# In the first attention, VectorE takes the low part of a step's transposed rows ahead of the maximum that belongs to two steps on

## The chip, the cores and the metric

The program runs on one core of one Trainium2 chip. A core has a matrix engine (PE, TensorE), a vector engine (DVE, VectorE), a scalar engine (ACT, ScalarE), GpSimd (POOL) and a queue engine (SP). Each works through its own list of instructions in order, and they wait for one another by semaphores. The metric is the device time of one execution in microseconds (us), median over runs; less is faster.

## The reference, cut to what matters

Two blocks follow one another on 512 tokens of width 1024, the first with 256 context tokens beside them. The change touches only the first attention of the first block, which has 8 heads, keys of 96 columns (64 computed for each head, 32 shared and rotated) and values of 64:

```python
def attention(q, k, v):
    ...
        s = jnp.einsum('bqhgd,bkhd->bhgqk', qi, k).astype(jnp.float32) * scale
        p = jax.nn.softmax(s, axis=-1).astype(v.dtype)
        return jnp.einsum('bhgqk,bkhd->bqhgd', p, v)

def mla_pool_mixer(hc, hl, w_in, g_q, w_uq, g_kv, w_uk, w_uv, w_pool, s_pool, w_out, cos, sin, need_ctx):
    ...
    al = attention(ql, jnp.concatenate([kc, kl], axis=1), jnp.concatenate([vc, vl], axis=1))
    ...
        ac = attention(qc, kc, vc)
```

The 512 main tokens attend to all 768 keys, the 256 context tokens to the 256 context keys. Everything is computed in 32-bit precision.

## The kernel before, in words

**Products in two parts.** Each 32-bit operand of a matmul is held as a high part, which ACT writes (`copy`, line 1317), and a low part, which DVE writes as the value less its high part (`low`, line 1866). `three` (lines 620 to 622) then makes three matmuls. Weight tiles (`RAW`) are split in the same way: ACT writes `WH`, DVE writes `WL` (`split`, line 1859). There are two slots for weight tiles, and PE waits until both parts of a tile are there (`tile_ready`).

**Steps.** The first attention has 8 heads (numbered 0 to 7 here) of 5 steps (0 to 4), 40 in all, counted by `w`. Step 0 of a head has the two query blocks of the context side by side (2 x 256 columns); steps 1 to 4 have 128 queries by 768 keys each. A step goes through these hands:

- `scores(w)` on PE, issued two steps ahead (in step w-2),
- `maximum(w)` on DVE (line 2120), also issued two steps ahead,
- `exps(w)` on ACT (line 1466), two steps ahead as well: it waits for the maximum,
- `prob(w)` on DVE, one step ahead: reciprocal of the sum (line 2126) and scaling (line 2129),
- `transposes(w)` on PE (line 841), then `pt_high_of(w)` on ACT and `pt_low(w)` on DVE, which copy the transposed rows out as high and low part (`PTA`),
- `values(x)` on PE with the finished rows, and `out_taken(x)` on ACT, which copies its result out (`OA_C`, `OA_M`).

**What else stands in the steps.** While one head runs, the next head's operands are made: in step 0 `context_products`, in step 1 the queries and their rotation (`query_rope` on DVE, four long instructions, lines 2073 to 2078), in step 2 the keys (`key_high`, `key_low`) and the halves of the rotated queries (`query_high` on ACT, behind `exps`; `query_low` on DVE), in steps 3 and 4 of odd heads the values. In steps 3 and 4 of even heads ACT and DVE split the two weight tiles of the next pair of heads; on both engines the split is the last thing of its step. In the odd head's step 0, `context_products` on PE waits for both tiles.

Beside that run pieces of the modulation (steps 2 and 4 of heads 0 to 6, steps 1 to 4 of head 7): PE makes `mod_rows` (line 634), DVE copies the sums out (`mod_take`, line 1871, tile `MROW`), PE turns them (`mod_turn`, line 642) and DVE adds them (`mod_add`, line 1876). On PE `mod_rows` stands ahead of the step's transposes and waits for an `out_taken`, since they share a PSUM bank; `mod_turn` stands behind the transposes, and the next step's `scores` stand behind it. The order on every engine is written out by hand.

ACT's order in a step is: `out_taken` (steps 1, 2 and 4), the copies for the next head, `pt_high_of(w)`, `exps(w + 2)`, then `query_high` (step 2) or the tile split (steps 3 and 4 of even heads).

Of the kernel before, what the change touches and what calls it, by code (L numbers as in the profile page):

```python
# [98 lines left out]
def build(nc, a, out):  # L99
# [118 lines left out]
    with ctx:  # L218
# [179 lines left out]
        MLA_UNITS = MLA_HEADS * MLA_STEPS  # L398
# [11 lines left out]
        def mla_row(w):  # L410
            return psf[:, 1024 * (w % 2) + TC:1024 * (w % 2) + 1024]
# [4 lines left out]
        def mla_pt(w, pt):  # L416

            n, x = w % MLA_STEPS, mla_x(w)
            flat = psf[:, 4 * 512:4 * 512 + (4 if n == 0 else 6) * P]
            if n == 0:  # L420
                return (pt[:, x % 2, 0:2, :].rearrange("p b (q n) -> p q b n", q=2), flat.rearrange("p (q b n) -> p q b n", q=2, b=2))
            q = (n - 1) % 2
            return pt[:, x % 2, :, q * P:(q + 1) * P], flat.rearrange("p (b n) -> p b n", b=6)
# [7 lines left out]
        def mla_widths(w):  # L431
            return (TC, TC) if w % MLA_STEPS == 0 else (TA,)
# [3 lines left out]
        def mla_mod_sums(bank):  # L436
            return PS[:, bank, 2 * P:4 * P]

        def mla_mod_col(bank):
            return PS[:, bank, 0:4]  # L440
# [1414 lines left out]
        def _(dve):  # L1855
            def split(s):

                dve.wait_ge(tile_hi, s.times(1, 1))
                dve.tensor_tensor(WL[:, s.mod(2), :], RAW[:, s.mod(2), :], f32(WH[:, s.mod(2), :]), ALU.subtract  # L1859
                                  ).then_inc(tile_split[s.mod(2)], 1)  # L1860
# [4 lines left out]
            def low(dst, src, high):  # L1865
                return dve.tensor_tensor(dst, src, f32(high), ALU.subtract)  # L1866

            def mod_take(j, sums=MOD_SUMS):

                dve.wait_ge(mod_done, j.times(2, 2))  # L1870
                dve.tensor_copy(MROW[:, :], sums).then_inc(mod_row, 1)

            def mod_add(j, col=MOD_COL):

                dve.wait_ge(mod_turned, j.times(1, 1))
                dve.tensor_tensor(MOD[:, j.ds(2, 2), :], col.rearrange("p (a v) -> p a v", a=2),
                                  COLS[:, j.ds(2, 2, COL["b_mod"])].unsqueeze(2).to_broadcast([P, 2, 2]), ALU.add).then_inc(mod_read, 1)
# [213 lines left out]
            def context_low(j):  # L2091
                dve.wait_ge(mla_ctx_hi, j + 1)
                low(QA[1][rows96, j % 2, 0:TC], PS[rows96, ctx_bank(j), 0:TC], QA[0][rows96, j % 2, 0:TC])
                low(KA[1][rows64, j % 2, 0:TC], PS[rows64, ctx_bank(j), TC:2 * TC], KA[0][rows64, j % 2, 0:TC]).then_inc(mla_ctx_read, 1)

            def key_low(j):
                dve.wait_ge(mla_k_hi, j + 1)
                low(KA[1][rows64, j % 2, TC:TA], PS[rows64, key_bank(j), :], KA[0][rows64, j % 2, TC:TA]).then_inc(mla_k_read, 1)

            def query_rope(j):  # L2100
                dve.wait_ge(mla_q_read, j + 1)
                if j:
                    dve.wait_ge(mla_q_ready, j)
                rope(At(1 + j), rows96, QRAW_A[rows96, :], RT[0][rows96], rope_done)

            def query_low(j):
                dve.wait_ge(mla_q_hi, j + 1)
                low(QA[1][rows96, j % 2, TC:TA], RT[0][rows96], QA[0][rows96, j % 2, TC:TA]).then_inc(mla_q_ready, 1)

            def value_low(pair, half):  # L2110
                dve.wait_ge(mla_v_hi, 2 * pair + half + 1)
                hi, lo = [x[:, 3 * half:3 * half + 3, :].rearrange("p b n -> p (b n)") for x in VA[pair % 2]]
                low(lo, value_bank(pair, half), hi).then_inc(mla_v_read, 1)

            def maximum(w):

                dve.wait_ge(score_done, w + 1)
                n = len(mla_widths(w))
                src = mla_row(w)[:, 0:sum(mla_widths(w))].rearrange("p (n k) -> p n k", n=n)
                dve.tensor_reduce(STAT[:, w % 2, 0:n], src, AX.X, ALU.max, negate=True).then_inc(row_max, 1)  # L2120

            def prob(w):

                dve.wait_ge(row_exp, w + 1)
                st, n, at = STAT[:, w % 2, :], len(mla_widths(w)), 0
                dve.reciprocal(st[:, 4:4 + n], st[:, 2:2 + n]).then_inc(row_recip, 1)
                dve.wait_ge(row_recip, w + 1)
                for m, width in enumerate(mla_widths(w)):
                    ins = dve.tensor_scalar(PROB[:, w % 2, at:at + width], PROB[:, w % 2, at:at + width], st[:, 4 + m:5 + m], None, ALU.mult)
                    at += width  # L2130
                ins.then_inc(row_prob, 1)

            def pt_low(w):
                dve.wait_ge(pt_hi, w + 1)
                hi, flat = mla_pt(w, PTA[0])
                lo, _ = mla_pt(w, PTA[1])
                low(lo, flat, hi).then_inc(pt_ready, 1)

            def out_low(i):
                dve.wait_ge(mla_out_hi, i + 1)  # L2140
                low(GC[1][:, i, :], OA_C[:, i, :], GC[0][:, i, :])
                low(GM[1][:, i, :], OA_M[:, i, :], GM[0][:, i, :]).then_inc(mla_out_ready, 1)
# [11 lines left out]
            for w in range(MLA_UNITS):  # L2154
                j, n = w // MLA_STEPS, w % MLA_STEPS
                more = j + 1 < MLA_HEADS
                if w + 1 < MLA_UNITS:
                    prob(w + 1)
                if w + 2 < MLA_UNITS:
                    maximum(w + 2)  # L2160
                if more:
                    if n == 0:
                        context_low(j + 1)
                    elif n == 2:
                        key_low(j + 1)
                    elif n >= 3 and j % 2:
                        value_low((j + 1) // 2, n - 3)
                if w in MLA_PAIR:
                    pair, bank = MLA_PAIR[w]
                    mod_take(At(pair), mla_mod_sums(bank))  # L2170
                pt_low(w)
                if w in MLA_PAIR:
                    mod_add(At(pair), mla_mod_col(bank))
                if more:
                    if n == 1:
                        query_rope(j + 1)
                    elif n == 2:
                        query_low(j + 1)
                    elif n >= 3 and j % 2 == 0:
                        split(At(TILES["mla"] + j + n - 1))  # L2180
                elif n < 3:
                    out_low(n)
# [634 lines left out]
```

## Time and profile before

| | us |
|---|---|
| median of 3 runs | 3115.05 |
| the three runs | 3099.72, 3115.77, 3115.05 |
| the profiled execution | 3100.32 |
| its span | 3098.6 |
| PE busy in the span | 2781.3 (90%) |
| DVE busy | 1625.6 (52%) |
| ACT busy | 1052.9 (34%) |
| steps of the first attention, from about 205 to 431 | 226 |

The profile is of one execution. A timeline row gives the start, the duration, the engine, the line, the operation and its tiles; in square brackets stands how long the engine sat idle before it and what ended that. Rows that follow at once on an engine overlap by a few hundredths, since a record runs from start to finish of a pipelined instruction. The whole first attention is 7% of the span; the rest of the program isn't touched.

### The profile page before, as it was taken

How to read it: one execution, taken by the hardware profiler on the slowest of the kernel's cores; microseconds unless marked ns; L12 is line 12 of the kernel's file. 1: busy time of each engine (PE TensorE's matmuls, PEld its weight loads, DVE VectorE, ACT ScalarE, POOL GpSimd, SP SyncE). 2: the span in 40 equal slices, each digit the busy share in tenths (PEclk: the TensorE clock that was granted, in tenths of full speed). 3: DMA queues.
4: the chain of work that ended last, by engine and by line, in shares of the span. 5: the costliest groups of instructions: out<-in, count | busy, mean ns of one | idle time of the engine just before them, and what ended most of it. 6: DMA issues, size and time to landing. Idle time of an engine off the chain costs nothing. (4 is left out here: it accounts for less than half of the span.)

```text
span 3098.6 us, 38172 instructions
## 1 busy us (share of the span) xinstructions
PE 2781.3 (90%) x14558; PEld 2236.1 (72%) x14558; DVE 1625.6 (52%) x2409; ACT 1052.9 (34%) x1620; POOL 82.0 (3%) x108
## 2 busy tenths in 40 slices
PE   5968987999999977887899997989997999999997
PEld 3857776888888866776677775777774777777775
DVE  5576645333333347675544445255555565555566
ACT  2144433222222223453333333333333333333343
POOL 0000110000000000000000000000000000000000
PEclk8989998999999998999899998989998999999999
DMA  5212231222222211001122222212221222222221
GB/s 202 68 55 83 82 116 54 96 96 88 95 95 88 95 62 41 29 21 55 61 89 88 88 88 102 90 63 78 81 81 56 82 84 84 84 77 84 84 77 41
DMA packets 67206, 246.41 MB, mean 80 GB/s; under 512 B 7505, under 2 KB 7889, under 8 KB 66385
## 3 DMA queue, kind: packets, MB, share of 16 engines
q1 hardware_dynamic: 51280, 185.10, 18.1%
q0 software_dynamic: 14768, 55.51, 5.4%
q10 hardware_dynamic: 1040, 4.12, 0.4%
q8 instruction: 89, 1.46, 0.2%
q14 instruction: 29, 0.23, 0.0%
HBM read 242.45 MB, written 2.24 MB: 79 GB/s over the span
## 5 line engine op out<-in xcount | busy, mean ns | idle before, releaser
L1859 DVE TENSOR_TENSOR WL<-RAW,WH 128x1024 fp32r<-128x1024 f32 x331 | 405.2, 1225 | 696.4 <-ACT WH L1317 693.9
L620 PE MATMUL PS<-HM,WH 128*128 128x512 f32 x1752 | 707.7, 404 | 32.4 <-DVE HM L1866 10.9
L621 PE MATMUL PS<-HM,WH 128*128 128x512 f32 x1752 | 700.3, 400 | 0.0
L622 PE MATMUL PS<-HM,WL 128*128 128x512 f32 x1752 | 698.6, 399 | 0.0
L1317 ACT ACTIVATE WH<-RAW 128x1024 fp32r<-128x1024 f32 x331 | 349.5, 1057 | 776.1 <-PE PS L622 765.9
L620 PEld LDWEIGHTS PS<-HM,WH 128*128 128x128 f32 x1752 | 333.4, 190 | 111.0 <-issue 32.3
L622 PEld LDWEIGHTS PS<-HM,WL 128*128 128x128 f32 x1752 | 333.4, 190 | 80.1
L621 PEld LDWEIGHTS PS<-HM,WH 128*128 128x128 f32 x1752 | 333.6, 190 | 55.1
L620 PE MATMUL PS<-GM,WH 128*128 128x512 f32 x468 | 192.0, 410 | 27.2 <-DVE GM L1866 15.5
L621 PE MATMUL PS<-GM,WH 128*128 128x512 f32 x468 | 191.4, 409 | 0.0
L622 PE MATMUL PS<-GM,WL 128*128 128x512 f32 x468 | 190.7, 407 | 0.0
L620 PE MATMUL PS<-HC,WH 128*128 128x256 f32 x448 | 132.6, 296 | 36.6 <-DVE HM L1918 28.9
L620 PEld LDWEIGHTS PS<-HC,WH 128*128 128x128 f32 x448 | 85.6, 191 | 73.5 <-issue 40.0
L622 PE MATMUL PS<-HC,WL 128*128 128x256 f32 x448 | 129.8, 290 | 0.0
L621 PE MATMUL PS<-HC,WH 128*128 128x256 f32 x448 | 127.9, 286 | 0.0
L620 PEld LDWEIGHTS PS<-GM,WH 128*128 128x128 f32 x468 | 92.0, 197 | 42.8 <-DVE GM L1866 18.2
L2193 DVE SCALAR_TENSOR_TENSOR X_M<-PS,MOD,X_M 128x512 f32<-128x512 f32 x112 | 83.5, 746 | 68.5 <-PE PS L622 68.5
L622 PEld LDWEIGHTS PS<-GM,WL 128*128 128x128 f32 x468 | 91.5, 196 | 22.1
L2193 DVE SCALAR_TENSOR_TENSOR X_C<-PS,MOD,X_C 128x256 f32<-128x256 f32 x56 | 27.1, 483 | 149.8 <-PE PS L622 149.8
L1866 DVE TENSOR_TENSOR PTA<-PS,PTA 128x768 fp32r<-128x768 f32 (+1 forms) x72 | 66.4, 923 | 71.7 <-ACT PTA L1317 71.6
L1773 ACT ACTIVATE PROB<-PROB,STAT 128x768 f32<-128x768 f32 x64 | 59.5, 931 | 128.7 <-DVE STAT L2553 128.7
L1317 ACT ACTIVATE PTA<-PS 128x768 fp32r<-128x768 f32 (+1 forms) x72 | 56.6, 787 | 125.9 <-PE PS L1040 80.4
(357 smaller groups left out, 4787.7 us busy)
## 6 DMA issues: line engine op xcount, KB each, us to landing
RAW<-in_tiles SPq DMA_DIRECT2D x333, 512.0 KB, 3.3
MRAW<-in_mods POOLq DMA_DIRECT2D x80, 512.0 KB, 4.6
TB<-bias_rows POOLq DMA_DIRECT2D x16, 576.0 KB, 6.3
FIRST<-in_mods SPq DMA_DIRECT2D x8, 1024.0 KB, 23.8
X_M<-in_x ACTq DMA_DIRECT2D x1, 2048.0 KB, 17.0
VN_GB<-in_gm_rows POOLq DMA_DIRECT2D x2, 1024.0 KB, 5.9
out_x<-X_M SPq DMA_DIRECT2D x8, 256.0 KB, 2.0
X_C<-in_ctx ACTq DMA_DIRECT2D x1, 1024.0 KB, 19.8
```

Of the source, the lines that this page charges most:

```text
L620: pe.matmul(out_, wh, xh, start=first, stop=False, skip_group_check=True)
L621: pe.matmul(out_, wh, xl, start=False, stop=False, skip_group_check=True)
L622: return pe.matmul(out_, wl, xh, start=False, stop=last, skip_group_check=True)
L1317: return act.activation(out_, in_, ACT.Copy, scale=scale)
L1773: act.activation(rows, rows, ACT.Exp, bias=STAT[:, h, 0:1], accum_out=STAT[:, h, 2:3]).then_inc(dil_exp, 1)
L1859: dve.tensor_tensor(WL[:, s.mod(2), :], RAW[:, s.mod(2), :], f32(WH[:, s.mod(2), :]), ALU.subtract).then_inc(tile_split[s.mod(2)], 1)
L1866: return dve.tensor_tensor(dst, src, f32(high), ALU.subtract)
L2193: return dve.scalar_tensor_tensor(out=xx, in0=src, scalar=MOD[:, col.ds(), v:v + 1].rearrange("p a v -> p (a v)"), in1=xx, op0=ALU.mult, o ...
```

## The change

`maximum(w + 2)` moves from behind `prob(w + 1)` to behind `pt_low(w)`. No instruction is added or removed, and only DVE's order changes.

```diff
@@ the loop over the steps, on VectorE @@
                 if w + 1 < MLA_UNITS:
                     prob(w + 1)
-                if w + 2 < MLA_UNITS:
-                    maximum(w + 2)
                 if more:
                     if n == 0:
                         context_low(j + 1)
...
                     mod_take(At(pair), mla_mod_sums(bank))
                 pt_low(w)
+                if w + 2 < MLA_UNITS:
+                    maximum(w + 2)
                 if w in MLA_PAIR:
                     mod_add(At(pair), mla_mod_col(bank))
```

VectorE's list in the first head, from `mod_take` of step 2 to the end of step 3. Line 2120 is the maximum, 1871 `mod_take`, 1866 with `PTA` is `pt_low`, 1866 with `QA` is `query_low`, 2126 and 2129 are `prob`, 1859 is the low part of a weight tile. Before:

```order
L1871 COPY MROW<-PS 128x256
L1866 TENSOR_TENSOR PTA_109<-PS,PTA_108 128x6x128
L1876 TENSOR_TENSOR MOD<-PS,COLS 128x4
L1866 TENSOR_TENSOR QA_107<-RT_113,QA_106 96x512
L2126 RECIPROCAL STAT<-STAT 128x1
L2129 TENSOR_SCALAR PROB<-PROB,STAT 128x768
L2120 TENSOR_REDUCE STAT<-PS 128x2
L1866 TENSOR_TENSOR PTA_109<-PS,PTA_108 128x6x128
L1859 TENSOR_TENSOR WL<-RAW,WH 128x1024
```

The same stretch after:

```order
L1871 COPY MROW<-PS 128x256
L1866 TENSOR_TENSOR PTA_109<-PS,PTA_108 128x6x128
L2120 TENSOR_REDUCE STAT<-PS 128x1
L1876 TENSOR_TENSOR MOD<-PS,COLS 128x4
L1866 TENSOR_TENSOR QA_107<-RT_113,QA_106 96x512
L2126 RECIPROCAL STAT<-STAT 128x1
L2129 TENSOR_SCALAR PROB<-PROB,STAT 128x768
L1866 TENSOR_TENSOR PTA_109<-PS,PTA_108 128x6x128
L2120 TENSOR_REDUCE STAT<-PS 128x2
L1859 TENSOR_TENSOR WL<-RAW,WH 128x1024
```

The maximum of step 4 (`128x1`) now stands between step 2's `pt_low` and `query_low`, and that of the next head's step 0 (`128x2`) between step 3's `pt_low` and the weight tile. Step 4 of the same head on VectorE, up to the reciprocal of the step that follows. Before:

```order
L2120 TENSOR_REDUCE STAT<-PS 128x1
L1871 COPY MROW<-PS 128x256
L1866 TENSOR_TENSOR PTA_109<-PS,PTA_108 128x6x128
L1876 TENSOR_TENSOR MOD<-PS,COLS 128x4
L1859 TENSOR_TENSOR WL<-RAW,WH 128x1024
```

After:

```order
L1871 COPY MROW<-PS 128x256
L1866 TENSOR_TENSOR PTA_109<-PS,PTA_108 128x6x128
L2120 TENSOR_REDUCE STAT<-PS 128x1
L1876 TENSOR_TENSOR MOD<-PS,COLS 128x4
L1859 TENSOR_TENSOR WL<-RAW,WH 128x1024
```

The maximum went from ahead of `mod_take` to between `pt_low` and the weight tile.

## Rows read from the trace of the kernel before

**Rows 1.** The head of the page.
```profile
span 3098.6 us, 38172 instructions
```
**Rows 2.** Waits of PE from 205 to 431: us in total, times, longest.
```profile
PE PS L642 <- DVE MROW L1871: 21.2, 12, 2.4
PE PS L620 <- issue: 4.5, 3, 1.6
```
**Rows 3.** Timeline of DVE in head 4, steps 1 and 2.
```profile
325.27 0.96 DVE L1866 TENSOR_TENSOR PTA<-PS,PTA 128x768 fp32r<-128x768 f32 x1 [2.68 <-ACT PTA L1317]
...
329.73 0.94 DVE L2120 TENSOR_REDUCE STAT<-PS 128x1 f32<-128x768 f32 x1
...
331.19 0.40 DVE L1871 COPY MROW<-PS 128x256 f32<-128x256 f32 x1
```
**Rows 4.** Timeline of PE in head 4, steps 2 to 4, and after.
```profile
331.64 0.61 PE L642 MATMUL PS<-CONST,MROW 128*128 128x2 f32 x4 [2.36 <-DVE MROW L1871]
...
338.43 1.04 PE L634 MATMUL PS<-MRAW,CVEC 128*2 128x256 f32 x16
...
344.38 0.33 PE L620 MATMUL PS<-CQ,WH 128*96 128x256 f32 x1 [1.59 <-issue]
```
**Rows 5.** Timeline of ACT in head 4, steps 2 to 4.
```profile
330.70 0.90 ACT L1466 ACTIVATE PROB<-PS,STAT 128x768 f32<-128x768 f32 x1 [0.51 <-DVE STAT L2120]
...
331.59 0.62 ACT L1317 ACTIVATE QA<-RT 96x512 fp32r<-96x512 f32 x1
...
335.82 0.47 ACT L1466 ACTIVATE PROB<-PS,STAT 128x256 f32<-128x256 f32 x1
...
336.71 1.06 ACT L1317 ACTIVATE WH<-RAW 128x1024 fp32r<-128x1024 f32 x1
337.66 0.37 ACT L1317 ACTIVATE OA_M<-PS 64x256 f32<-64x256 f32 x1
340.38 0.81 ACT L1317 ACTIVATE PTA<-PS 128x768 fp32r<-128x768 f32 x1 [2.35 <-PE PS L841]
341.09 0.89 ACT L1466 ACTIVATE PROB<-PS,STAT 128x768 f32<-128x768 f32 x1
...
341.96 1.05 ACT L1317 ACTIVATE WH<-RAW 128x1024 fp32r<-128x1024 f32 x1
```
**Rows 6.** Timeline of DVE in head 4, steps 2 to 4.
```profile
332.45 0.67 DVE L1866 TENSOR_TENSOR QA<-RT,QA 96x512 fp32r<-96x512 f32 x1
...
333.23 0.62 DVE L2129 TENSOR_SCALAR PROB<-PROB,STAT 128x768 f32<-128x768 f32 x1
333.77 0.69 DVE L2120 TENSOR_REDUCE STAT<-PS 128x2 f32<-128x512 f32 x1
335.95 0.96 DVE L1866 TENSOR_TENSOR PTA<-PS,PTA 128x768 fp32r<-128x768 f32 x1 [1.49 <-ACT PTA L1317]
...
343.05 1.23 DVE L1859 TENSOR_TENSOR WL<-RAW,WH 128x1024 fp32r<-128x1024 f32 x1 [0.80 <-ACT WH L1317]
```
**Rows 7.** Timeline of head 0: `mod_take` of step 2, and PE's next context products.
```profile
216.78 0.41 DVE L1871 COPY MROW<-PS 128x256 f32<-128x256 f32 x1
...
228.41 0.33 PE L620 MATMUL PS<-CQ,WH 128*96 128x256 f32 x1 [1.32 <-issue]
```
**Rows 8.** Timeline of DVE in head 3, step 4.
```profile
313.46 0.56 DVE L1866 TENSOR_TENSOR VA<-PS,VA 128x384 fp32r<-128x384 f32 x1 [1.52 <-ACT VA L1317]
313.94 0.42 DVE L1871 COPY MROW<-PS 128x256 f32<-128x256 f32 x1
```
**Rows 9.** Stretches: length; busy PE, PEld, DVE, ACT, POOL; PEclk; DMA share; GB/s.
```profile
327.50:331.60 4.10, 1.78 (x22) 0.88 (x22) 4.02 (x8) 2.30 (x5) 1.44 (x2) 1.00 0.35 107
332.10:335.50 3.40, 3.40 (x18) 3.40 (x18) 2.33 (x6) 0.50 (x2) 0.00 (x0) 0.51 0.33 129
```
**Rows 10.** Timeline of PE in head 7, steps 2 and 3.
```profile
410.67 1.89 PE L634 MATMUL PS<-MRAW,CVEC 128*2 128x256 f32 x16 [0.15 <-ACT OA_C L1317]
...
416.19 0.61 PE L634 MATMUL PS<-MRAW,CVEC 128*2 128x256 f32 x8 [1.75 <-DMA MRAW<-in_mods]
```

## The prediction

> **What bounds the kernel now.** The profiled execution took 3100.3 us, its span is 3098.6 [rows 1]. I read the waits of PE over the first attention first, because PE is the busiest engine and because what follows the attention starts when PE is through with it. Its largest wait there is for `MROW`, the sums that `mod_take` on DVE copies out: 21.2 us in 12 waits [rows 2]. The second is called "issue", 4.5 us in three waits of up to 1.6. In the timeline such a wait stands ahead of the context products that follow an even head [rows 4] (at 344.38), and it ends 0.10 after DVE's low part of the second weight tile (343.05 + 1.23 = 344.28) [rows 6]. It is a wait for that tile. So in even heads two things of DVE hold PE: `mod_take` and the tile.
>
> **What the change seems to offer, and why it isn't there.** Before, a maximum (0.86 us in a queue, 0.94 less the overlap with its neighbour) stands ahead of `mod_take`, and PE waits 2.36 us for `mod_take` in step 2 of a head [rows 3, 4]. Taking the maximum out should give 0.86 in each of seven heads. But follow DVE back from that `mod_take`. It worked without a gap from the low part of step 1, which itself began after 2.68 us of idleness, when ACT's high part was done (at 325.27) [rows 3]. Between this anchor and `mod_take` stand the rotation, `prob`, one maximum (at 329.73) and the low part of the keys. After the change the maximum of step 2 is gone from there, but that of step 1, which used to lie in the 2.68 us of idleness, now comes right behind the low part of step 1. One maximum leaves and one enters: `mod_take` of step 2 stays where it is. Gain 0, in all seven heads with this pattern.
>
> **What it costs: `exps` comes behind two more instructions.** Before, ACT took `exps(w+2)` directly behind its high part, since the maximum was long there (the high part at 340.38 ends at 341.19, `exps` starts at 341.09) [rows 5]. Now DVE first takes the low part (0.88) and then the maximum (0.87), and everything behind `exps` in ACT's list comes later: `query_high` in step 2, the tile in steps 3 and 4, `out_taken` of the next step. The low parts on DVE wait for the first two, and `mod_rows` on PE waits for the last. I follow this from the end of `mod_take` in step 2 of head 4 (331.59) to PE's context products:
>
> - low part of step 2, 0.88, and maximum, 0.86 [rows 3, 6]: 1.74
> - `exps` and `query_high` on ACT, from 330.70 to 332.21 in [rows 5], and 0.03 to begin: 1.54
> - `query_low` on DVE [rows 6]: 0.70; `prob`, from the end of the former at 333.12 to 333.85: 0.73
> - low part of step 3, 0.88, and the two-part maximum, 0.69 less 0.08 [rows 6]: 1.49. The low part would start at 336.3; the high part that it needs was there at 335.95 in this trace [rows 6], so DVE's queue is what counts.
> - `exps`, tile and `out_taken` on ACT, from 335.82 to 338.03 [rows 5]: 2.24. This is the place that I consider the heart of it: `mod_rows` of step 4 on PE waits for this `out_taken`.
> - `mod_rows`, transposes, high part: from 338.43 [rows 4] to 341.19 [rows 5], and 0.05: 2.81
> - low part of step 4, 0.99, and maximum, 0.87: 1.86
> - `exps` and tile on ACT, from 341.09 to 343.01 [rows 5]: 1.95
> - low part of the tile, 1.27, and 0.10 to PE: 1.37
>
> The sum is 16.43 us. Before, the same stretch took 344.38 - 331.59 = 12.79 in head 4, and in head 0 228.41 - 217.19 = 11.22 [rows 7]. Head 0 is quicker because PE's clock was not at half there, as it was in head 4 from 332.1 to 335.5 [rows 9]; the new chain runs mostly through ACT and DVE, so I take it as the same 16.43 for both. Cost: 5.2 in head 0, 3.6 in head 4, and 3.6 in head 2, which shows the same tile wait. Together 12.5. Within it PE's `mod_turn` of step 4 comes some 1.2 later than before; that is part of the sum, not beside it.
>
> **Odd heads** have no tile in steps 3 and 4. DVE waits there for the values from PE and ACT, 1.52 us before 313.46, and `mod_take` follows that [rows 8]. The moved maximum and the later `exps` (about 1.9 us) fit ahead of it: 0, at most 0.5 in each of three heads.
>
> **Head 6 and head 7.** After head 6 no context products follow, so PE doesn't wait for a tile but, in head 7, for `out_taken` behind ever later `exps`. At least one low part and one maximum go on the path: 1.8. At most, `mod_rows` of step 2 moves by 5.4 (from 410.67 [rows 10], by the same adding up: 3.6 from the tile of head 6, the rest from low part and maximum in steps 0 and 1). It now waits for ACT's copy by only 0.15. Behind it PE waits 1.75 for a transfer of modulation weights that is issued when `mod_rows` frees the buffer, so that moves too, and is not a cover. Since the slow clock there (1.89 for rows that take 1.04 elsewhere) may fall away, I take 4.5.
>
> **The clock.** In head 4 PE was busy 1.78 of 4.10 us from 327.5 to 331.6, and in the 3.4 us from 332.1 the granted clock was half, 1.2 instead of 2.4 GHz [rows 9]. The new wait for the tile leaves PE empty from about 343.9 to 348.0, as long a stretch and with less work in it. Such a period costs at most half of its 3.4 us, 1.7, where PE is the bound, as it is in the context products and step 0 after. None in three places is 0, all three is 5.1; I take 4, nearer to the upper end because the row of the trace is a milder case of the same. The Trainium skill says the same of idle gaps ("TensorE: Matmul & The Clock Gate", section "HAM oscillation — how this bites in real kernels"): short bursts with waits between them are run at the lower clock again and again. By that rule the term would be the whole 5.1, and a stretch of step 4 that has much waiting in it would add to it; that is the third rival below.
>
> **Sum.** 12.5 + 4.5 + 4 = 21 us, all of it lost: 3121 against the profiled 3100.3. The three runs shown are 3099.7, 3115.1 and 3115.8, so the profile is one of the low kind, and the median is 14.8 above it. Nothing in one trace tells what these 15 us are. I add the 21 to the median: **3136**. If the new kernel's median falls on the low kind, it is 3121.
>
> **The rivals.**
>
> 1. *Only the last link counts.* If `out_taken` doesn't hold PE in step 4 (because `mod_rows` is late anyway), each even head loses only low part and maximum ahead of the tile, 1.86, and the last pair about as much: 4 x 1.9 = 8 us, 3108 to 3123. For it speaks that before, `out_taken` ended 0.4 ahead of `mod_rows` and held nothing; against it that the chain above needs 2 us more than that. Chance 0.17.
>
> 2. *Faster.* If DVE reached the low part of step 1 late rather than waiting for it, the maximum that leaves the front of `mod_take` would be a gain: 0.86 in seven heads, 0.7 in step 4 of three, 0.86 in head 7, together about 9 us, 3106. It decides at the idleness ahead of the low part of step 1: above 0.9 us there is nothing to win, and the trace has 2.68. Chance 0.05, and less than that for a gain of over 0.5%.
>
> 3. *The clock costs more.* If each even head gets two more periods at half speed in which PE is the bound, instead of hardly one, 4 x 2 x 1.7 = 14 takes the place of 4: 31 us, 3146. Against it speaks that only the context products and what follows lie behind the long gap, and that the half-speed period inside the new chain is hidden by ACT and DVE. Chance 0.12.
>
> 4. *Nothing that can be seen*, since waits elsewhere take it up: 3100 to 3115. After the attention PE goes from product to product, so I see no such place. Chance 0.08.
>
> **How the numbers follow.** The forecast has 0.58. The range takes in its own span (12 to 26 us on the lower or the higher kind), rival 1 on the lower kind (3108) and rival 3 on the higher with a little over it: 3108 to 3150. A measurement can tell a change from none from about 0.5%, 15.5 us. Faster by that is a part of rival 2: 0.04. Within it fall rivals 1, 4 and what is left of 2, and the lower edge of the forecast: 0.31. Slower: 0.65.
>
> **What would show it.** In the profile after: `mod_take` of step 2 still ends 6.3 us after the start of the low part of step 1 (331.59 - 325.27), with the maximum now right behind that low part. PE's rows of `mod_rows` in step 4 of even heads are released by ACT's `OA_M`. The "issue" wait ahead of the context products grows from 1.6 to about 4, and the stretch from `mod_take` to these products takes 16.4 in heads 0, 2 and 4 alike. `exps` on ACT shows waits for the maximum in every step. Odd heads keep their length. I would be wrong if step 2's wait for `MROW` fell to 1.5 (rival 2), or if `mod_rows` of step 4 started right behind the scores as before (rival 1).

## The result, and the profile after

| | before | after |
|---|---|---|
| median of 9 runs, us | 3108.19 | 3124.88 |
| lowest to highest | 3099.72 to 3115.77 | 3116.51 to 3129.20 |
| ratio | | 1.0050, 95% interval 1.0033 to 1.0066 |
| span of the profiled execution | 3098.6 | 3127.5 |
| first attention: from the first transposes of head 0 to the first output product | 225.6 (205.38 to 431.02) | 250.6 (209.75 to 460.30) |

The changed kernel is slower by 10 to 20 us. The two profiled executions differ by 28.9 us, of which 24.9 lie in the first attention and 4.4 in front of it, where nothing was changed (head 0 starts at 209.75 instead of 205.38). The ratios below leave out one execution of the kernel `rows_late`, of 5091.5 us at a granted clock of 0.83; its others have 0.95.

The waits of PE over the attention of the changed kernel (us in total, times, longest), which answer to [rows 2]:

```profile
PE PS L634 <- ACT OA_M L1317: 11.1, 5, 3.1
PE PS L620 <- issue: 10.8, 3, 4.1
PE PS L642 <- DVE MROW L1871: 9.0, 9, 1.2
PE PS L634 <- ACT OA_C L1317: 7.8, 8, 1.1
PE PS L634 <- DVE MOD L1876: 2.6, 1, 2.6
```

The wait for `MROW` fell from 21.2 to 9.0, which looks like success. But two waits that were hardly there have taken its place, for ACT's output copies `OA_M` and `OA_C` (18.9 together, all ahead of `mod_rows`), and the wait for the weight tile ("issue") went from 4.5 to 10.8. The last row is one wait in head 7, where `mod_rows` of step 3 needs `mod_add` of step 2, which now stands behind the maximum. In all PE stood idle for 44.6 of the 250.6 us (30.6 of 225.6 before), and was busy for 205.9 (195.1 before) with the same instructions, at a mean granted clock of 0.87 (0.93 before). So by PE's rows 14.0 of the 24.9 us are waiting and 10.9 are slower matmuls.

VectorE in head 2, steps 1 and 2 (start, duration, then what it was), which answers to [rows 3, 6]:

```profile
281.71 0.96 DVE L1866 TENSOR_TENSOR PTA<-PS,PTA 128x768 fp32r<-128x768 f32 x1 [1.95 <-ACT PTA L1317]
282.58 0.95 DVE L2120 TENSOR_REDUCE STAT<-PS 128x1 f32<-128x768 f32 x1
...
286.86 0.68 DVE L1866 TENSOR_TENSOR KA<-PS,KA 64x512 fp32r<-64x512 f32 x1
287.46 0.41 DVE L1871 COPY MROW<-PS 128x256 f32<-128x256 f32 x1
287.79 0.94 DVE L1866 TENSOR_TENSOR PTA<-PS,PTA 128x768 fp32r<-128x768 f32 x1
288.65 0.94 DVE L2120 TENSOR_REDUCE STAT<-PS 128x1 f32<-128x768 f32 x1
...
291.17 0.69 DVE L1866 TENSOR_TENSOR QA<-RT,QA 96x512 fp32r<-96x512 f32 x1 [1.51 <-ACT QA L1317]
```

A maximum now follows each low part. From the start of step 1's low part to the end of `mod_take` it is 287.87 - 281.71 = 6.16 us, against 6.32 before: one maximum left this stretch and one came in, and `mod_take` didn't come sooner. Behind `mod_take` DVE now waits 1.51 for ACT's `query_high`.

ACT in the same head, steps 3 and 4 (against [rows 5]):

```profile
294.09 0.47 ACT L1466 ACTIVATE PROB<-PS,STAT 128x256 f32<-128x256 f32 x1 [2.25 <-DVE STAT L2120]
...
295.00 1.05 ACT L1317 ACTIVATE WH<-RAW 128x1024 fp32r<-128x1024 f32 x1
295.95 0.37 ACT L1317 ACTIVATE OA_M<-PS 64x256 f32<-64x256 f32 x1
298.32 0.81 ACT L1317 ACTIVATE PTA<-PS 128x768 fp32r<-128x768 f32 x1 [2.00 <-PE PS L841]
301.02 0.90 ACT L1466 ACTIVATE PROB<-PS,STAT 128x768 f32<-128x768 f32 x1 [1.89 <-DVE STAT L2120]
```

The exponents, which used to follow the high part of these steps without a gap, now wait 1.9 to 2.3 us for DVE's maximum, and the tile and the output copy stand behind them. On PE (against [rows 4]) this becomes:

```profile
296.37 1.05 PE L634 MATMUL PS<-MRAW,CVEC 128*2 128x256 f32 x16 [1.61 <-ACT OA_M L1317]
297.35 0.88 PE L841 MATMUL PS<-IDENT,PROB 128*128 128x128 f32 x6
298.43 0.61 PE L642 MATMUL PS<-CONST,MROW 128*128 128x2 f32 x4 [0.20 <-DVE MROW L1871]
304.32 0.50 PE L620 MATMUL PS<-CQ,WH 128*96 128x256 f32 x1 [4.13 <-issue]
```

`mod_rows` of step 4 starts 0.05 after `OA_M` is copied out (296.32), and the context products wait 4.13 us for the tile.

The heads one by one, in the changed kernel (length; busy PE, PEld, DVE, ACT, POOL with counts; granted clock; DMA share; GB/s). Heads 0 to 5:

```profile
209.75:241.99 32.24, 23.77 (x154) 19.02 (x153) 19.84 (x36) 13.30 (x26) 3.05 (x4) 0.82 0.29 98
241.99:274.23 32.24, 30.11 (x208) 26.31 (x207) 18.05 (x34) 12.51 (x26) 2.94 (x4) 0.85 0.16 54
274.23:307.60 33.37, 25.30 (x172) 20.70 (x171) 20.45 (x38) 14.21 (x29) 3.08 (x4) 0.88 0.32 107
307.60:336.34 28.74, 26.60 (x207) 22.80 (x207) 17.86 (x34) 12.53 (x26) 2.94 (x4) 0.97 0.17 60
336.34:371.14 34.80, 26.27 (x173) 20.81 (x172) 20.53 (x38) 14.20 (x29) 3.09 (x4) 0.80 0.29 103
371.14:398.97 27.83, 25.70 (x209) 21.90 (x207) 17.77 (x34) 12.41 (x26) 2.95 (x4) 1.00 0.18 63
```

and heads 2 to 5 of the kernel before:

```profile
259.81:288.22 28.41, 23.71 (x173) 19.27 (x172) 20.50 (x37) 13.40 (x27) 2.88 (x4) 0.94 0.33 112
288.22:317.79 29.57, 27.21 (x208) 23.48 (x207) 18.38 (x36) 12.72 (x27) 2.88 (x4) 0.94 0.22 75
317.79:346.20 28.41, 23.72 (x173) 19.27 (x172) 20.46 (x37) 13.39 (x27) 2.88 (x4) 0.94 0.32 112
346.20:375.78 29.58, 27.21 (x209) 23.49 (x207) 18.38 (x36) 12.72 (x27) 2.88 (x4) 0.94 0.20 71
```

Heads 2 and 4 became 5.0 and 6.4 us longer, and head 0 7.4 (24.84 before). The odd heads don't move together: head 1 became 2.6 us longer (29.59 before), at a clock of 0.85 instead of 0.94, and head 5 1.75 us *shorter* than its 29.58 before, at 1.00. The clock column holds something that the waits don't show, and that the experiments had to take apart.

### The profile page after: what moved, and what is told of

Read it like the earlier page. It is cut to its first block and busy times, and to the rows that moved or that the text cites. A ratio compares the mean times of both kernels' runs of the same rounds, so it can differ in the third digit from the quotient of the medians.

```text
span 3127.5 us, 38172 instructions
## 1 busy us (share of the span) xinstructions
PE 2796.4 (89%) x14558; PEld 2245.8 (72%) x14558; DVE 1624.7 (52%) x2409; ACT 1055.7 (34%) x1620; POOL 82.8 (3%) x108
## 3 DMA queue, kind: packets, MB, share of 16 engines
HBM read 242.45 MB, written 2.24 MB: 78 GB/s over the span
## 5 line engine op out<-in xcount | busy, mean ns | idle before, releaser
L620 PE MATMUL PS<-HM,WH 128*128 128x512 f32 x1752 | 707.3, 404 | 32.4 <-DVE HM L1866 10.9
L620 PEld LDWEIGHTS PS<-HM,WH 128*128 128x128 f32 x1752 | 333.1, 190 | 111.3 <-issue 32.6
L620 PE MATMUL PS<-HC,WH 128*128 128x256 f32 x448 | 132.6, 296 | 36.6 <-DVE HM L1918 28.9
L620 PEld LDWEIGHTS PS<-GM,WH 128*128 128x128 f32 x468 | 91.8, 196 | 42.8 <-DVE GM L1866 18.2
L2193 DVE SCALAR_TENSOR_TENSOR X_C<-PS,MOD,X_C 128x256 f32<-128x256 f32 x56 | 27.1, 483 | 149.6 <-PE PS L622 149.6
L621 PEld LDWEIGHTS PS<-GM,WH 128*128 128x128 f32 x468 | 91.4, 195 | 10.3
```

The source lines that it names most:

```text
L620: pe.matmul(out_, wh, xh, start=first, stop=False, skip_group_check=True)
L621: pe.matmul(out_, wh, xl, start=False, stop=False, skip_group_check=True)
L2193: return dve.scalar_tensor_tensor(out=xx, in0=src, scalar=MOD[:, col.ds(), v:v + 1].rearrange("p a v -> p (a v)"), in1=xx, op0=ALU.mult, o ...
```

## The experiments

Each kernel was timed against the kernel before. The ratio and its 95% interval stand with each.

**Both kernels again.** No edit. First the kernel before.

> The kernel before, unchanged, to see a second profile of it. If its 15 us of spread come from the start of the program and from where the half-speed periods of PE's clock fall, this profile shows the same waits in the first attention (21 us for MROW, 4.5 us for the tile), and differs from the first in the time ahead of it and in the number of half-speed periods. Ratio 1.000.

Ratio 0.9992 (0.9981 to 1.0003). The profiled execution has a span of 3111.4, 12.8 above the other profile of the same program. Head 0 starts at 210.71, 5.3 later, and the attention takes 233.0 instead of 225.6, with nearly the same waits (20.3 for `MROW`, 5.2 for the tile). The difference in the attention is the clock:

```profile
235.56:268.10 32.54, 30.18 (x208) 26.45 (x207) 18.56 (x36) 12.72 (x27) 2.88 (x4) 0.84 0.19 68
```

This is head 1 with a clock of 0.84, 3 us longer than head 3 above, which has the same instructions. 5.3 + 7.3 = 12.6 of the 12.8 us: between these two profiles, the spread that the prediction left open is the time ahead of the attention and the number of half-speed periods in it.

> The changed kernel, unchanged, for a second profile. My theory (the softmax's exponents come behind a low part and a maximum, and with them ACT's copy and tile): from the end of mod_take in step 2 to the context products again 16.4 to 17.1 us in heads 0 and 2 (11.2 and 12.8 before), and the first attention longer by 17 us plus a share for the clock of 0 to 10 that varies from run to run. If the loss were the clock alone, the stretch would come near 12.8 wherever the clock is at full speed. Ratio 1.003 to 1.007.

Ratio 1.0061 (1.0042 to 1.0081), attention 251.0, waits as in the first profile (10.8 for the tile, 11.1 for `OA_M`). From `mod_take` of step 2 to the context products it takes 235.42 - 218.18 = 17.2 us in head 0 and 300.88 - 284.45 = 16.4 in head 2. The second is the sum to the tenth, against 12.8 before (286.40 - 273.60): the loss isn't the clock alone.

**The move in odd heads only.**

```diff
-                if w + 2 < MLA_UNITS:
+                late = j % 2 == 1 and more
+                if w + 2 < MLA_UNITS and not late:
                     maximum(w + 2)
...
                 pt_low(w)
+                if w + 2 < MLA_UNITS and late:
+                    maximum(w + 2)
```

> The move is made in heads 1, 3 and 5 alone, the rest is as before. My theory: no cost and no gain, since DVE waits for the values there and mod_take of step 2 hangs on the low part of step 1: 0 us, within 1 us in the attention, and the wait for MROW in step 2 stays at 2.4 less what PE waits ahead of mod_rows. Rival (the maximum ahead of mod_take was the cost): 0.86 less in each of three heads, -2.6 us. Rival (any move costs): +3 to +4 us each, +10.

Ratio 0.9968 (0.9956 to 0.9979): some 10 us *faster* than before. None of the three sums foresaw that. The attention took 218.5 us in the profile, 7.1 less than in the first profile of before and 14.5 less than in the second. Heads 1 to 4 of this kernel:

```profile
235.65:263.49 27.84, 25.71 (x208) 21.91 (x207) 17.77 (x34) 12.41 (x26) 2.94 (x4) 1.00 0.22 78
263.49:290.33 26.84, 22.15 (x172) 17.70 (x171) 20.50 (x38) 14.08 (x29) 2.89 (x4) 1.00 0.35 115
290.33:318.18 27.85, 25.72 (x209) 21.92 (x208) 17.77 (x34) 12.41 (x26) 2.94 (x4) 1.00 0.22 78
318.18:345.01 26.83, 22.14 (x173) 17.69 (x172) 20.48 (x38) 14.08 (x29) 2.89 (x4) 1.00 0.35 117
```

The granted clock is 1.00 in these and in heads 5 and 6, and even heads, which have the old order, are 1.6 us shorter as well (26.84 against 28.41). Against the first profile of before, heads 1 to 6 are 1.1 to 1.8 us shorter each, 9.5 in sum; head 0, at 0.94, is 1.8 longer. So the gain isn't a wait that went away: over the attention PE was idle for 31.7 us (30.6 before), and busy for 186.8 instead of 195.1. In six of the heads it no longer fell to half speed.

**The move in even heads only**, with `late = j % 2 == 0` in the same edit.

> The move is made in heads 0, 2, 4 and 6 alone. My theory: nearly the whole loss is here. 12.5 to 15 us up to the context products of heads 0, 2 and 4, 2.5 to the start of head 7, 0 to 8 for the clock, and little in head 7, whose own steps are as before: +16 to +22 us, some 2 less than the whole change. Rival (the loss lies in all heads alike): four sevenths of it, about +10.

Ratio 1.0087 (1.0068 to 1.0105): +27 us, above the 16 to 22 expected and more than the whole change costs. Its waits for the tile and `OA_M` are close to those of the changed kernel (10.8 and 9.6; there 10.8 and 11.1), and PE was idle for 44.1 us in all (there 44.6) and busy for 211.5 (there 205.9). Heads 1, 3 and 5, in the old order, take 32.3, 32.0 and 32.6 us at clocks of 0.84 to 0.87, where the changed kernel has 32.2, 28.7 and 27.8. So +27 from the even heads and -10 from the odd ones make the +17 of the change.

**Late rows, and no maximum moved.** What differs for PE in odd heads is where it waits around `mod_rows` of step 2. Before, `mod_rows` and the transposes came at once and a wait of 2.36 for `MROW` followed. With the move there are a wait of 1.07 for `OA_C`, then the matmuls, then 1.05. This kernel makes the same pattern in the old order:

```diff
+                    if n == 2 and j % 2 and j + 1 < MLA_HEADS:
+                        pe.wait_ge(rope_step, 3 * (j + 2) + 3)
                     if bank == 6:
                         pe.wait_ge(o_read, 3 * j + n // 2)
```

> The kernel before, with one wait more: in step 2 of heads 1, 3 and 5 PE starts mod_rows only when the third instruction of the rotation on VectorE is done, some 0.8 us later, inside the time that it then waits for mod_take. No maximum moves. Theory A (the 10 us that the move in odd heads gained came from where PE's clock falls to half, which the pause ahead of mod_rows changes): the half-speed period in each of heads 1 to 6 is gone here too, heads are 26.8 and 27.8 us long, and the time is 7 to 10 us below before. Theory B (the gain came from the place of the maximum itself): 0 us, heads of 28.4 and 29.6 us as before.

Ratio 0.9968 (0.9953 to 0.9983), the same as `odd_heads`. A wait *added* to PE made the kernel 10 us faster. Head 1 in step 2 of `odd_heads`:

```profile
246.45 1.04 PE L634 MATMUL PS<-MRAW,CVEC 128*2 128x256 f32 x16 [1.07 <-ACT OA_C L1317]
247.43 0.88 PE L841 MATMUL PS<-IDENT,PROB 128*128 128x128 f32 x6
249.36 0.61 PE L642 MATMUL PS<-CONST,MROW 128*128 128x2 f32 x4 [1.05 <-DVE MROW L1871]
```

and of this kernel, whose line numbers behind the edit are 2 higher (L2078 is the third instruction of the rotation here, L1873 `mod_take`):

```profile
246.36 1.04 PE L634 MATMUL PS<-MRAW,CVEC 128*2 128x256 f32 x16 [0.75 <-DVE RT L2078]
247.34 0.87 PE L841 MATMUL PS<-IDENT,PROB 128*128 128x128 f32 x6
249.60 0.61 PE L642 MATMUL PS<-CONST,MROW 128*128 128x2 f32 x4 [1.39 <-DVE MROW L1873]
```

PE was idle for 30.7 us of this kernel's attention, as before (30.6), and busy for 188.8 instead of 195.1. So theory A holds for where the time comes from. Its forecast for each head doesn't: heads 1, 2, 5 and 6 were at 1.00, but heads 3 and 4 at 0.94 (29.4 and 28.4 us). And the divided wait doesn't decide it by itself. In head 3 of this kernel the waits are the same 0.75 and 1.39, and the clock falls to half 3 us later:

```profile
301.05 1.04 PE L634 MATMUL PS<-MRAW,CVEC 128*2 128x256 f32 x16 [0.75 <-DVE RT L2078]
304.29 0.61 PE L642 MATMUL PS<-CONST,MROW 128*128 128x2 f32 x4 [1.39 <-DVE MROW L1873]
307.50:310.50 3.00, 3.00 (x16) 3.00 (x16) 0.83 (x2) 1.61 (x4) 0.00 (x0) 0.50 0.02 5
```

In head 2 of `odd_heads` the wait stands undivided, as before, and the clock stays at full speed:

```profile
277.35 0.61 PE L642 MATMUL PS<-CONST,MROW 128*128 128x2 f32 x4 [2.36 <-DVE MROW L1871]
277.40:280.80 3.40, 3.40 (x29) 3.40 (x30) 3.15 (x7) 1.78 (x5) 0.00 (x0) 1.00 0.47 174
```

Both edits in odd heads make the half-speed periods rarer; how, these runs don't show.

**Even heads with late rows**: both edits above.

> even_heads (the move in heads 0, 2, 4 and 6, +27 us) together with the late rows of rows_late (PE's pause of 0.8 us ahead of mod_rows in step 2 of heads 1, 3 and 5, no maximum moved there, -10 us alone). If the odd heads' part of the change is its effect on PE's clock and nothing else, this kernel behaves as the changed one: +15 to +20 us, odd heads of 27.8 us where no half-speed period falls. If the maximum's place in odd heads has an effect of its own: +27.

Ratio 1.0065 (1.0040 to 1.0089), +20 us, between 12 and 28. The kernel with the move in even heads alone has 1.0087; the two intervals overlap, so the times alone don't settle it. The one trace shows head 5 at 27.85 us, as in the changed kernel (27.83), while heads 1 and 3 stay at 32.2 and 31.9 (changed kernel: 32.2 and 28.7). In this trace the pause gives back part of what the maximum's move in odd heads gives back; whether it does so in the median, and whether all of it, stays open.

**The output copy first.** The changed kernel, with ACT's copy moved ahead of the exponents of step 3 in even heads:

```diff
-                elif n in (2, 4):
+                elif n == 2 or n == 4 and j % 2:
                     out_taken(3 * j + n // 2 - 1)
...
                 pt_high_of(w)
+                if n == 3 and j % 2 == 0:
+                    out_taken(3 * j + 1)
```

> The changed kernel, and in even heads ACT takes the output copy of step 4 in step 3, ahead of the exponents, so that mod_rows of step 4 doesn't stand behind exponents and tile. If this copy is the whole gate of step 4: the context products come 2.5 to 3 us sooner in each even head, about -11 us against the changed kernel. By the sums that I now make from the trace after, VectorE's own queue (low part of the tile, prob, mod_take) is next: -0.8 to -1.4 per even head, -3 to -5 us against the changed kernel (about +13 against before), with no wait of PE for OA_M in step 4 and a wait for MROW in its place.

Ratio 1.0033 (1.0016 to 1.0050), about 9 us below the changed kernel by the medians, more than the 3 to 5 that I summed. In head 2:

```profile
283.51 1.04 PE L634 MATMUL PS<-MRAW,CVEC 128*2 128x256 f32 x16
284.48 0.87 PE L841 MATMUL PS<-IDENT,PROB 128*128 128x128 f32 x6
288.70 1.01 PE L642 MATMUL PS<-CONST,MROW 128*128 128x2 f32 x4 [3.35 <-DVE MROW L1873]
293.71 0.50 PE L620 MATMUL PS<-CQ,WH 128*96 128x256 f32 x1 [1.86 <-issue]
```

`mod_rows` waits for nothing now, and the wait turned into 3.35 us for `MROW`: DVE takes the tile's low part and `prob` ahead of `mod_take`, as foreseen. From the head's first transposes to the context products it is 29.2 us, against 30.1 in the changed kernel (head 2), and 27.4 against 29.0 in head 0: -0.9 and -1.6 on the path, the size of the sum. Most of the rest lies in head 1, 28.2 us instead of 32.2 at a clock of 0.99 instead of 0.85: the clock again.

**The tile first.** The changed kernel, with the tile's high part ahead of the exponents on ACT:

```diff
                 pt_high_of(w)
+                if j + 1 < MLA_HEADS and j % 2 == 0 and n >= 3:
+                    split(At(TILES["mla"] + j + n - 1), (mla_q_done if n == 3 else mla_k_done, j + 2))
                 if w + 2 < MLA_UNITS:
                     exps(w + 2)
...
-                    elif j % 2 == 0 and n >= 3:
-                        split(At(TILES["mla"] + j + n - 1), (mla_q_done if n == 3 else mla_k_done, j + 2))
```

> The changed kernel, and on ACT the weight tile of steps 3 and 4 of even heads stands ahead of the exponents. VectorE's order is that of the changed kernel. If exponents behind low part and maximum are what delays the tile: mod_rows of step 4 0.9 sooner, the tile's low part behind the maximum without a wait, the context products 3 to 3.4 us sooner in heads 0, 2 and 4: -10 us against the changed kernel or more where the clock stays up, so +5 to +9 against before. If the tile's way is not what counts: no change against the changed kernel.

Ratio 1.0016 (1.0001 to 1.0031), 10 to 14 us below the changed kernel. The context products follow the head's first transposes after 25.3 us in head 0 (29.0 in the changed kernel) and 27.1 in head 2 (30.1): -3.7 and -3.0, against 3 to 3.4 summed. The exponents behind low part and maximum are what delays the tile. In this profile heads 1, 3 and 5 all take 32.2 to 32.3 us at a clock of 0.85; in the changed kernel heads 3 and 5 took 28.7 and 27.8. Half of what the even heads win is lost again there.

**The way that the traces point to.** From the kernel before, not from the change: the maximum stays, and `mod_take` goes forward. In step 2 it stands ahead of `prob`, and in step 4 of even heads and in head 7 ahead of the maximum:

```diff
+                if more and n == 2:
+                    take()
                 if w + 1 < MLA_UNITS:
                     prob(w + 1)
+                if not more or n == 4 and j % 2 == 0:
+                    take()
                 if w + 2 < MLA_UNITS:
                     maximum(w + 2)
...
-                    elif n == 2:
-                        key_low(j + 1)
...
                 pt_low(w)
+                if more and n == 2:
+                    key_low(j + 1)
```

This alone (`take` calls `mod_take` where the step has a piece of the modulation; step 4 of odd heads keeps its old place). "The last version" and `take_and_tile_first` in its expectation are the version with both parts, which was built first and stands further down:

> The kernel before, with VectorE's part of the last version alone: mod_take first in step 2 (the keys' low part behind the step's low part), and ahead of the maximum in step 4 of even heads and in head 7; ACT as before. If PE's wait for MROW was the main cost that is to be had: -14 to -18 us against before. If the tile on ACT carried the gain of take_and_tile_first: -3 to -6.

Ratio 0.9989 (0.9973 to 1.0006): nothing, and neither forecast, though PE's 21.2 us of waiting for `MROW` fell to 1.2. In their place PE waits 5.0 for low parts ahead of transposes, 4.9 for the keys' low part and 7.3 for the tile, so that it was idle for 26.6 us instead of 30.6. The clock fell in every head of the profile (0.85 to 0.97), and in heads 1, 2 and 5 below the 0.94 of before.

ACT's part alone, the tile ahead of the exponents:

> The kernel before, with ACT's part alone: the tile of steps 3 and 4 of even heads ahead of the exponents; VectorE as before. The wait for the tile falls from 1.6 by 0.9 (one exponent of 0.9) in heads 0, 2 and 4: -2.7 us. With it the half-speed periods move, which can add -8 to +4; I expect -3 and would not be surprised by -8. If the tile was not on the path: 0.

Ratio 1.0007 (0.9992 to 1.0022): nothing either; its odd heads are 32.6 to 32.7 us long, as head 1 in the second profile of before.

Both together:

> Not the change but what the traces point to: the maximum stays where it was before, mod_take goes first in step 2 (ahead of prob, with the keys' low part behind the step's low part) and ahead of the maximum in step 4 of even heads and in head 7, and ACT splits the tile of steps 3 and 4 ahead of the exponents. PE's wait for MROW in step 2 falls from 2.4 to about 0.1 and the tile wait from 1.6 to below 0.8. Expected from before: -2.3 in each of three odd heads, -2 in each of four even heads, -1 in head 7, and the half-speed periods behind the long wait gone: -16 to -25 us. If mod_take was only a cover for other waits: 0 to -5.

Ratio 0.9944 (0.9926 to 0.9962), -17 to -21 us. The parts don't add up (0 and 0 make -17). In the profiles PE's idle time in the attention fell by 4.0 and 1.5 us with the parts and by 7.8 with both, while its busy time rose by 7.4 and 10.6 with the parts and fell by 0.9 with both. So it was slower matmuls that took up what the parts won. Since the second profile of before is also 7.1 us busier than the first, single profiles can't divide the 17 us more finely. Of the waits that were left (5.0 for low parts ahead of transposes, 5.0 for the tile, 4.9 for the keys' low part, 4.0 for a transfer) I took the 4.9, which are one wait of 1.62 in each odd head. With `key_low` ahead of the maximum in odd heads:

```diff
+                if more and n == 2 and j % 2:
+                    key_low(j + 1)
                 if w + 2 < MLA_UNITS:
                     maximum(w + 2)
...
-                if more and n == 2:
+                if more and n == 2 and j % 2 == 0:
                     key_low(j + 1)
```

> take_and_tile_first, but in odd heads the keys' low part stands ahead of the maximum and of the step's low part, since PE waits 4.9 us in three waits for it there (the values share its PSUM bank). Expected: these 4.9 us go, the transposes of step 3 in odd heads don't wait for the low part, since 2 us of values stand ahead of them: -4 to -5 against take_and_tile_first, -22 to -25 against before. If the transposes come to wait instead: 0 to -2 against take_and_tile_first.

Ratio 0.9914 (0.9884 to 0.9944), 3081.9 against 3105.8 us: the fastest version, 24 us below the kernel before and some 43 below the changed one. That is 7 to 9 us below `take_and_tile_first`, more than the 4 to 5 that were summed. The attention took 206.1 us. Heads 1 and 2:

```profile
232.64:258.50 25.86, 25.82 (x207) 22.00 (x207) 17.98 (x36) 12.75 (x27) 2.88 (x4) 1.00 0.19 65
258.50:283.48 24.98, 22.20 (x172) 17.74 (x171) 20.11 (x37) 13.43 (x27) 2.88 (x4) 1.00 0.36 117
```

Heads 3 and 4 are the same to 0.04 us. In head 1 PE is busy for all but 0.04 of the 25.86 us. Over the whole attention it was still idle for 16.9 us, 5.0 of them for the tile.

## Why the prediction was right, and where it was off

**The direction and the size.** Forecast was 3136 (3108 to 3150) and slower; measured were 3124.88 and a ratio of 1.0050 and, in the second comparison, 1.0061. Added to the median that was known then (3115.05) the 21 us gave 3136; over the nine runs of before the median is 3108.19, and the increase is 16.7 and 17.6 us in the two. So 7 us of the 11 that the forecast is too high are the base, and 4 the sum.

**The gain that isn't there.** The step said that one maximum leaves the front of `mod_take` and one enters. It ends 6.16 us after the start of step 1's low part, 6.32 before. Right. What the wait for `MROW` lost went to `OA_C` in front of `mod_rows`: 0.94 and 1.20 in head 2 in the place of 2.36. So the sign that I had set for being wrong, a wait of 1.5 for `MROW` in step 2, was a bad one: the wait fell to 1.20 without any gain. The prediction named `out_taken` as late only for step 4 and head 7; that it is late in step 2 of all heads, hidden behind the wait for `mod_take`, I did not write.

**The chain in even heads.** Summed 16.43 us; head 2 of the changed kernel, piece by piece, with the ends taken from the rows above and their neighbours:

| piece | summed | head 2 |
|---|---|---|
| low part and maximum, step 2 (to 289.59) | 1.74 | 1.72 |
| exponents and `query_high` (to 291.14) | 1.54 | 1.55 |
| `query_low` (to 291.86) and `prob` (to 292.59) | 1.43 | 1.45 |
| low part and maximum, step 3 (to 294.06) | 1.49 | 1.47 |
| exponents, tile, output copy (to 296.32) | 2.24 | 2.26 |
| `mod_rows`, transposes, high part (to 299.13) | 2.81 | 2.81 |
| low part and maximum, step 4 (to 300.99) | 1.86 | 1.86 |
| exponents and tile (to 302.96) | 1.95 | 1.97 |
| the tile's low part, to PE (304.32) | 1.37 | 1.36 |
| sum | 16.43 | 16.45 |

In head 0 it was 17.1 (238.70 - 221.59) and in head 4 17.95 (367.94 - 349.99). There PE's part ran at half speed (in head 4 `mod_rows` took 1.89 instead of 1.04, and in both heads the transposes 1.54 instead of 0.88). I had taken the new chain as free of PE's clock, 16.4 in heads 0, 2 and 4 alike. It is not, since 1.9 of its microseconds are PE's at full speed. The extra of heads 0, 2 and 4 is then 5.9 + 3.6 + 5.2 = 14.7 instead of 12.5.

**Heads 6 and 7.** Taken as 4.5. In the trace 2.5 us were lost from `mod_take` in step 2 of head 6 (389.57, then 412.61) to the first transposes of head 7 (10.99, then 13.52), and 3.7 in head 7 (30.46, then 34.17): 6.2. `OA_C` and `OA_M` released PE as described, with waits of 0.90 and 0.96 in steps 2 and 1 of head 7, but there was a third that the prediction doesn't have: the 2.59 for `mod_add`. `mod_add` too stands behind the moved maximum; before, PE waited 1.75 for the transfer at the same place.

**The odd heads, and the clock: here the step failed.** "0, at most 0.5 in each" for odd heads, which "keep their length", and +4 for the clock. The waits of the odd heads are as the sum has them (in head 5 PE was idle for 2.1 us, 2.4 before). Their lengths are not: 32.2, 28.7 and 27.8 us instead of 29.6. But I asked only where the change would *add* a half-speed period, and took the one that each head had before ([rows 9]) as given. It costs some 1.6 to 1.75 us a head, and the move in odd heads takes it away in most of them: -10 us in `odd_heads`. In turn the even heads lose more to the clock than the 4 us: +27 in `even_heads`, where chain and last heads of the changed kernel's trace account for 20.9. That the sum of the two comes near the forecast is luck. In the trace of the changed kernel the stretches from the context products to the next `mod_take` of step 2 changed by +4.0, +0.5 and -0.5, in sum the 4 us that I took. Their total was right by cancelling, which is luck too: the first holds several half-speed periods more, and the last one less.

**The rivals.** Rival 1 (only the last link counts, +8) is out: `mod_rows` waits for `OA_M`, and the chain is as long as summed. Rival 2 (a gain from the maximum) is out in its mechanism: the gain that odd heads did bring came just as well without moving the maximum. Rival 3 (two more half-speed periods for each even head, +14 in the place of 4) is nearer the truth for the even heads than the forecast: in `even_heads` PE was busy for 16.5 us more than before. It was offset by the odd ones, which no rival had. Rival 4 is out: the median lies 16.7 us above that of before.

The page of the Trainium skill that I drew on ("TensorE: Matmul & The Clock Gate", section "HAM oscillation — how this bites in real kernels") ties the fall to waits of an idle PE. The trace agrees for the waits of over 3 us, behind all of which the clock is at half in the changed kernel. In head 2 of the changed kernel the granted clock is 1.00 up to 302.20, in the middle of the wait of 4.13 for the tile, and 0.50 behind it (304.40 to 307.80). In heads 0 and 4 it fell earlier than the prediction has it, at the waits of 3.07 and 3.08 for `OA_M` ahead of `mod_rows` of step 4 (0.50 over 231.10 to 234.50 and 358.50 to 361.50), and it was at 0.50 through the wait for the tile (234.50 to 238.60, 364.00 to 367.90), which is 3.32 there and not 4. It doesn't cover the rest: in the kernel before the clock fell in heads whose longest wait is 2.36. The same wait stands in even heads of `odd_heads`, where it didn't fall, and in `rows_late` it fell in head 3, where the wait is divided, and not in head 1, where it is divided alike. Why the clock falls in one head and not in another is left open here.

## What to carry to other kernels

When an instruction is moved out of a queue's front, look for the anchor behind which the queue works without a gap: if an instruction of the same kind enters between anchor and goal, nothing is won. And follow the instruction's own consumer: here the maximum feeds the exponents, and ACT's tile and output copy stand behind these. To serve a waiting engine, move what it waits for (`mod_take`) forward, rather than something else backward, and then go to the next named wait: the parts gave 0 and 0 by themselves, -17 us together, and -24 with one wait more removed. Where the granted clock moves as in these traces, set the engine's busy time beside its idle time in each profile, and time every step, since an edit can cost or give 10 us without a wait in the trace that says so.

## What the runs showed of the hardware that I had not expected

- A wait of 0.8 us added to PE in three heads made the kernel 10 us faster (0.9968), with PE's idle time unchanged (30.7 against 30.6): in its profile the granted clock was 1.00 in four of the six heads where it was 0.93 or 0.94 before.
- The same program's attention took 225.6 and 233.0 us in two profiled executions with nearly the same waits (30.6 and 30.8 us of PE idle); the clock over head 1 was 0.94 in one and 0.84 in the other. Differences of 5 to 10 us between single profiles of this kernel say nothing by themselves.
- Half-speed periods often repeat from head to head. In the first profile of before heads 1 to 6 have one each (28.41 and 29.57 us for heads 2 and 3), in that of `odd_heads` none (26.84 and 27.85), so that an edit in odd heads alone switched the even ones too. It is no rule: `rows_late` has both kinds in one profile, with identical instructions in heads 1 and 3.
